# Summing eight expert rows: six on TensorE and two on VectorE, in place of four and four

## The chip, the cores and the metric

The kernel runs on one core of a Trainium2 chip. The time is the device time of one execution in microseconds (us), here the median of three. A core has several engines that run their own instruction streams and wait for each other through semaphores: TensorE (PE in the profile; its weight loads are PEld) multiplies matrices into PSUM, VectorE (DVE) and ScalarE (ACT) work element by element, GpSimd (POOL) does the gathers and scatters, and SyncE (SP) issues most of the transfers, which 16 DMA engines carry out.

## The reference

Two decoder layers over 272 tokens (16 learned meta tokens and 256 of the sequence) of width 1024. Layer 0 mixes tokens with an RWKV-7 recurrence, layer 1 with sliding-window attention. Behind each stands a mixture of experts: 64 routed ones of which every token uses 8, and a shared one. What the change touches is the end of that mixture and the norm behind it, cut to its core:

```
y = expert(x2d[tok], w_gate[e], w_up[e], w_down[e]) * gate      # 8 rows of 1024 for every token
routed = segment_sum(y, slot_tok, num_segments=T)               # their sum for every token
f = swiglu(x2d, sh_gate, sh_up, sh_down) + routed
h = layer_norm(DEEPNORM_ALPHA * h + f, ln_ffn_g[i], ln_ffn_b[i])
```

All of it is float32.

## The kernel before

The tokens stand in three tiles: tile 0 and tile 1 of 128 tokens, and a few, 16, in tile 2. Each layer runs its token mixer, then routing, then the 64 experts one after the other (their weights, 3 MB each, streamed from HBM by SyncE's queue), then the combine, which the change touches. There is no scheduler: each engine's instructions are written out in order, one block for each engine, and `Steps` objects (`end_pe`, `end_dve`, `end_act` for the combine) count what an engine has finished, so that another can wait for a named step.

The combine of a layer begins when the last scaled expert row has been scattered to a table in HBM, `routed`, with eight rows of 1024 for every token, side by side. SyncE then loads the few tokens' rows (line 1268), and for tile 0 and tile 1 the eight rows of each token in four loads of two rows each (line 1272, semaphores `routed_loaded{tile}_{pair}`): pair 0 holds rows 0 and 1, pair 3 rows 6 and 7. The eight loads are issued together, tile 0's four first. They go into the buffers `rt[t]`, which lie in the big SBUF buffer `arena`. The running sum of a tile is `h[:, t, :]`, which already holds the scaled input and the shared expert's part.

TensorE first sums the few tokens' rows (line 1851), then, for tile 0 and tile 1, adds up rows by products with the unit matrix `ident`, in two halves of 512 columns that gather in two PSUM banks for each tile (line 1857). Which rows those are is given by `ON_PE`, here rows 0, 1, 3 and 5; each row waits for its pair. The product of the last row raises the step `sum{t}` for each half.

VectorE adds the few tokens' sum and norms that tile, then takes tile 0 and tile 1 in turn: the rows of `ON_DVE_FIRST` (2 and 4) are added to `h` one after the other (line 2705, 128x1024), then the two halves from PSUM (line 2714, 128x512 each), then the rows of `ON_DVE_LAST` (6 and 7, both in pair 3), then the norm of the tile (`norm_tile`: two statistics passes on line 2683, mean and variance on 2686, two passes over the tile on 2688 and 2693; ScalarE gives the square root on line 2213). In layer 1 SyncE stores each normed tile to the output (lines 1277 to 1281), and the program ends. In layer 0 everything of layer 1's attention waits for the last norm: TensorE's transposes of `h` (line 1874, each followed by VectorE's copy on line 2732), its projections (line 1883, then line 1899 in groups, whose results ScalarE reads on lines 2250 and 2251), and the DMAs that ScalarE issues for the attention's bias (lines 2225 and 2236). SyncE's loads of the attention's weights (line 1234) do not wait for the norm, its loads of layer 1's first expert weights (line 834) do.

Of the kernel before, what the change touches and what calls it, by code (L numbers as in the profile page):

```python
# [123 lines left out]
def hybrid_trunk(nc, I, out):  # L124
    with ExitStack() as ctx:
# [3 lines left out]
        def sem(name):  # L129
            return ctx.enter_context(nc.semaphore(name))  # L130
# [18 lines left out]
        def view(at, *shape, rows=P, dt=None):  # L149
            n = int(np.prod(shape))  # L150
            assert at + n <= ARENA, (at, n)
            v = arena[0:rows, at:at + n]
            if dt is not None:
                v = v.bitcast(dt)
            if len(shape) == 2:
                v = v.rearrange("p (a b) -> p a b", a=shape[0])
            if len(shape) == 3:
                v = v.rearrange("p (a b c) -> p a b c", a=shape[0], b=shape[1])
            return v
# [93 lines left out]
        def ln_steps(t, halves=True):  # L253
# [29 lines left out]
                  for l in range(2)]  # L283
# [4 lines left out]
                            ("top8", 3), ("taken", 3), ("sel", 1), ("g0", 1), ("gsum", 1), ("g1", 1), ("g2", 1),  # L288
                            ("kr", 1), ("dest", 3), ("posm", 1), ("max", 1), ("maxi", 1), ("sm0", 1), ("sm1", 1),
                            ("sd", 6)]) for l in range(2)]  # L290
        ON_PE, ON_DVE_FIRST, ON_DVE_LAST = (0, 1, 3, 5), (2, 4), (6, 7)
        NORM = ("st0", "st1", "mv", "sub", "rec", "out")

        def norm_steps(t):
            return [(f"{n}_{t}", 1) for n in NORM]

        end_act = [Steps(sem(f"combine_act{l}"), [("std2", 1), ("std0", 1), ("std1", 1)]) for l in range(2)]
        end_pe = [Steps(sem(f"combine_pe{l}"), [("few", 2), ("sum0", 2), ("sum1", 2)]) for l in range(2)]
        end_dve = [Steps(sem(f"combine_dve{l}"), [("few", 2)] + norm_steps(2) + [("sum0", 6)] + norm_steps(0)
                         + [("sum1", 6)] + norm_steps(1)) for l in range(2)]  # L300


        NK = [128, 256, 272]
# [367 lines left out]
        few = view(16896, D)  # L671
# [1635 lines left out]
        def _(dve):  # L2307
# [280 lines left out]
            def moe(l):  # L2588
# [89 lines left out]
                def norm_tile(t):  # L2678

                    n = TILES[t][1]  # L2680
                    acc = h[0:n, t, :]
                    for half in range(2):
                        V.bn_stats(stat[0:n, t, 6 * half:6 * half + 6], acc[:, 512 * half:512 * half + 512])\
                            .then_inc(*es.step(f"st{half}_{t}"))
                    dve.wait_ge(*es.at(f"st1_{t}"))
                    V.bn_aggr(mv[0:n, t, :], stat[0:n, t, :]).then_inc(*es.step(f"mv_{t}"))
                    dve.wait_ge(*es.at(f"mv_{t}"))
                    V.scalar_tensor_tensor(out=acc, in0=acc, scalar=mv[0:n, t, 0:1], in1=lnrow[0:n, 0, :],
                                           op0=ALU.subtract, op1=ALU.mult).then_inc(*es.step(f"sub_{t}"))
                    dve.wait_ge(*end_act[l].at(f"std{t}"))  # L2690
                    V.reciprocal(rstd[0:n, t:t + 1], std[0:n, t:t + 1]).then_inc(*es.step(f"rec_{t}"))
                    dve.wait_ge(*es.at(f"rec_{t}"))
                    V.scalar_tensor_tensor(out=h[0:n, t, :], in0=acc, scalar=rstd[0:n, t:t + 1], in1=lnrow[0:n, 1, :],
                                           op0=ALU.mult, op1=ALU.add).then_inc(*es.step(f"out_{t}"))

                norm_tile(NT - 1)
                for t in range(NT - 1):
                    acc = h[:, t, :]
                    u = 0

                    def add(k):
                        dve.wait_ge(routed_loaded[t][k // 2], 16 * (l + 1))
                        if u:
                            dve.wait_ge(*es.at(f"sum{t}", u - 1))
                        V.tensor_tensor(acc, acc, rt[t][:, k, :], ALU.add).then_inc(*es.step(f"sum{t}", u))  # L2705

                    for k in ON_DVE_FIRST:
                        add(k)
                        u += 1
                    dve.wait_ge(*es.at(f"sum{t}", u - 1))  # L2710
                    for half in range(2):
                        dve.wait_ge(*end_pe[l].at(f"sum{t}", half))
                        cs = slice(512 * half, 512 * half + 512)
                        V.tensor_tensor(acc[:, cs], acc[:, cs], ps[:, 2 * t + half, :], ALU.add)\
                            .then_inc(*es.step(f"sum{t}", u))
                        u += 1
                    for k in ON_DVE_LAST:
                        add(k)
                        u += 1
                    dve.wait_ge(*es.at(f"sum{t}"))  # L2720
                    norm_tile(t)
                dve.wait_ge(*es.end())

            moe(0)


# [80 lines left out]

            dve.wait_ge(*av.end())
            moe(1)


# [24 lines left out]
```

## Time and profile before

| | |
|---|---|
| median of 3 runs | 1638.23 us (1637.66 to 1640.96) |
| the profiled execution | 1638.7 us, of which the span from first to last instruction is 1637.0 us |
| TensorE busy | 1454.8 us (89%) |
| VectorE busy | 614.0 us (38%) |
| ScalarE busy | 318.5 us (19%) |
| mean granted TensorE clock | 0.968 of full speed |
| HBM traffic | 329 GB/s over the span |

A busy share is a mean over stages with different limits, so a stage is read by its own timeline: which instruction there starts last, and what released it. In a row of the timeline the first figure is the start from the beginning of the span and the second how long the merged instructions took together; x16 means sixteen of them; the brackets give the idle time of the engine ahead of it and what ended it. TensorE's clock has two levels; 1.00 is 2.4 GHz and 0.50 is 1.2 GHz.

### The profile page before, as it was taken

To read this page: it belongs to the slowest core of one execution; us is meant where nothing else is said; L and a number is where in the kernel's file an instruction comes from. 1 tells how busy PE (TensorE), PEld (TensorE's weight loads), DVE (VectorE), ACT (ScalarE), POOL (GpSimd) and SP (SyncE) were. 2 spreads that over 40 slices of the span, in tenths; PEclk is the share of its full clock that TensorE was granted. 3 is DMA by queue.
4 is the path that set the end of the run, shared out by engine and by line. 5 is a ranking of instruction groups with operands and counts; after the bars stand their busy time and mean duration, and the time that the engine had idled before them with its cause. 6 is when DMAs were issued, how large, how long until landed. Compare 5 with 4: busy or idle time off the path is not lost.

```text
span 1637.0 us, 33339 instructions
## 1 busy us (share of the span) xinstructions
PE 1454.8 (89%) x12808; PEld 943.1 (58%) x12808; DVE 614.0 (38%) x1580; ACT 318.5 (19%) x743; POOL 328.2 (20%) x404
## 2 busy tenths in 40 slices
PE   6989988899999988888886698999999888888884
PEld 4776877656566655555553267565666555555541
DVE  5362352673333333223321704543333333333326
ACT  1621333110111111111111015111111111111110
POOL 6012000011232222222222120112322222222210
PEclk9999988899999999999999899999999999999997
DMA  7330002685999999999997995439999999999986
GB/s 201 125 116 1 4 4 80 221 324 198 414 412 412 415 416 415 415 415 415 415 415 292 370 294 206 146 126 415 413 414 414 416 414 415 415 415 416 414 346 251
DMA packets 139878, 508.42 MB, mean 311 GB/s; under 512 B 29273, under 2 KB 58273, under 8 KB 104188
## 3 DMA queue, kind: packets, MB, share of 16 engines
q1 hardware_dynamic: 103312, 456.49, 70.0%
q0 software_dynamic: 22288, 41.89, 7.1%
q10 hardware_dynamic: 14172, 8.54, 1.9%
q8 instruction: 77, 1.26, 0.3%
q14 instruction: 29, 0.24, 0.0%
HBM read 501.38 MB, written 36.90 MB: 329 GB/s over the span
## 4 chain that ended last, share of the span: by engine, by line
PE 46%; SPq 33%; DMA 8%; DVE 6%; issue 3%; ACTq 3%; ACT 1%; POOL 0%; POOLq 0%; DVEq 0%
SPq L834 33%; PE ps L782 10%; DMA arena<-in_moe_w_up 6%; PE ps L1466 6%; PE ps L800 5%; PE ps L1596 3%; ACTq L2225 3%; PE ps L763 2%; PE ps L1014 2%; PE ps L2001 2%; PE ps L770 2%; PE ps L1024 1%; DMA arena<-routed 1%; DVE h L2705 1%; PE ps L789 1%
## 5 line engine op out<-in xcount | busy, mean ns | idle before, releaser
L782 PE MATMUL ps<-arena 128*64 128x256 f32 x2752 | 316.2, 382 | 61.2 <-DMA arena<-in_moe_w_up 49.5
L782 PEld LDWEIGHTS ps<-arena 128*64 128x64 f32 x2752 | 214.2, 137 | 193.6 <-issue 126.5
L775 DVE COPY arena<-ps 128x512 f32<-128x512 f32 x128 | 88.5, 692 | 471.7 <-PE ps L770 471.7
L819 POOL DMA_INDIRECT arena<-hrows,arena x128 | 130.4, 1019 | 568.1 <-DVE arena L815 555.1
L782 PE MATMUL ps<-ring,arena 128*64 128x256 f32 x1344 | 153.5, 381 | 26.1 <-DMA ring<-in_moe_w_up 24.5
L824 POOL DMA_INDIRECT routed<-arena x128 | 117.3, 917 | 246.0 <-DVE arena L948 226.9
L800 PE MATMUL ps<-arena 128*64 128x512 f32 x688 | 166.6, 605 | 0.0
L948 DVE TENSOR_SCALAR arena<-ps,arena 64x512 f32<-64x512 f32 x128 | 95.1, 743 | 167.7 <-PE ps L800 167.7
L782 PEld LDWEIGHTS ps<-ring,arena 128*64 128x64 f32 x1344 | 99.8, 137 | 93.8 <-issue 36.4
L902 ACT COPY arena<-ps 128x256 f32<-128x256 f32 x128 | 47.7, 373 | 488.2 <-PE ps L782 488.2
L912 ACT ACTIVATE arena<-ps,arena 64x512 f32<-64x512 f32 x128 | 87.6, 684 | 208.2 <-PE ps L800 208.2
L763 PEld LDWEIGHTS ps<-arena 128*128 128x128 f32 (+1 forms) x768 | 105.6, 190 | 6.1 <-issue 2.3
L763 PE MATMUL ps<-arena 128*128 (+3 forms) x768 | 105.8, 242 | 2.1 <-DVE arena L815 2.1
L770 PE MATMUL ps<-ident,arena 128*128 128x128 f32 x512 | 83.8, 286 | 0.0
L770 PEld LDWEIGHTS ps<-ident,arena 128*128 128x128 f32 x512 | 53.8, 141 | 48.7 <-issue 48.5
L800 PE MATMUL ps<-ring,arena 128*64 128x512 f32 x336 | 81.3, 604 | 0.0
L800 PEld LDWEIGHTS ps<-arena 128*64 128x64 f32 x688 | 41.8, 136 | 63.5 <-issue 63.5
L1466 PE MATMUL ps<-arena,ring 128*128 128x272 f32 x256 | 64.2, 416 | 8.3 <-DVE arena L2379 4.4
L807 DVE SCALAR_TENSOR_TENSOR arena<-arena 128x384 f32<-128x384 f32 x128 | 69.2, 542 | 0.1
L906 ACT ACTIVATE arena<-ps 128x128 f32<-128x128 f32 x128 | 35.5, 278 | 152.4 <-PE ps L789 152.4
L1466 PEld LDWEIGHTS ps<-arena,ring 128*128 128x128 f32 x256 | 51.9, 203 | 20.4 <-DVE arena L2379 4.5
L789 PE MATMUL ps<-ident,arena 128*128 128x128 f32 x256 | 55.8, 299 | 1.0 <-issue 1.0
(360 smaller groups left out, 1532.8 us busy)
## 6 DMA issues: line engine op xcount, KB each, us to landing
arena<-in_moe_w_down SPq DMA_DIRECT2D x86, 1024.0 KB, 24.2
arena<-in_moe_w_gate SPq DMA_DIRECT2D x86, 1024.0 KB, 24.7
arena<-in_moe_w_up SPq DMA_DIRECT2D x86, 1024.0 KB, 24.8
ring<-in_moe_w_gate SPq DMA_DIRECT2D x42, 1024.0 KB, 24.6
ring<-in_moe_w_up SPq DMA_DIRECT2D x42, 1024.0 KB, 24.5
ring<-in_moe_w_down SPq DMA_DIRECT2D x42, 1024.0 KB, 24.3
arena<-routed SPq DMA_DIRECT2D x16, 1024.0 KB, 14.7
ring<-in_attn_w_qkv SPq DMA_DIRECT2D x6, 1024.0 KB, 16.4
```

Of the source, the lines that this page charges most:

```text
L763: mm = nc.tensor.matmul(dst[:, 0:3], hot[0:n, t, :], vals[0:n, t, :], start=(t == 0), stop=(t == NT - 1))
L770: mm = nc.tensor.transpose(dst[:, P * j:P * j + P], rows[:, P * j:P * j + P], ident[:, :])
L775: return nc.vector.tensor_copy(xgT.rearrange("p (r j) m -> p j r m", r=2), ps[:, bU, :].rearrange("p (j r m) -> p j r m", j=4, r=2))
L782: mm = nc.tensor.matmul(dst[SLOTS * j:SLOTS * j + SLOTS, 0:FF], xgT[:, k, :], slots[pair[j]][:, FF * k:FF * k + FF], start=(k == 0), stop= ...
L789: mm = nc.tensor.transpose(dst[:, P * j:P * j + P], guc[:, P * j:P * j + P], ident[:, :])
L800: mm = nc.tensor.matmul(dst[SLOTS * half:SLOTS * half + SLOTS, :], hid[:, j, :], slots[s][:, D * j + 512 * half:D * j + 512 * half + 512], ...
L819: return nc.gpsimd.indirect_dma_start(out=dst, out_offset=None, in_=hrows_d[l], in_offset=bass.IndirectOffsetOnAxis(ap=index, axis=0), bou ...
L824: return nc.gpsimd.indirect_dma_start(out=routed[l], out_offset=bass.IndirectOffsetOnAxis(ap=index, axis=0), in_=src, in_offset=None, boun ...
L834: sp.dma_start(slot_view(s, j), expert_weights(l, num(e))[j]).then_inc(slot_loaded[s], 16)
L912: nc.scalar.activation(ysc[q[1] % 2][:, 512:1024], ps[SLOTS:P, bY[q[1] % 2], :], ACT.Copy, scale=gate_s[q[1] % INDICES][SLOTS:P]).then_inc ...
L948: nc.vector.tensor_scalar(ysc[q[1] % 2][:, 0:512], ps[0:SLOTS, bY[q[1] % 2], :], gate_s[q[1] % INDICES][0:SLOTS], None, ALU.mult).then_inc ...
L1466: m = mm_(b[:, 0:T], slot3(s)[:, k, P * (c % 2):P * (c % 2) + P], xm[MIXBUF[mix]][:, k, :], start=(k == 0), stop=(k == KC - 1))
```

## The change

`ON_PE` becomes rows 2 to 7 and VectorE adds rows 0 and 1, both of pair 0, ahead of the halves from PSUM; nothing is added behind them, so the norm follows the halves directly. The eight loads and their order stay as they are. The number of steps that VectorE counts for a tile goes from six to four. Both layers' combines change alike. Below line 2713 the lines of the changed kernel are numbered three lower than before.

```
-        ON_PE, ON_DVE_FIRST, ON_DVE_LAST = (0, 1, 3, 5), (2, 4), (6, 7)
+        ON_PE, ON_DVE = (2, 3, 4, 5, 6, 7), (0, 1)
...
-        end_dve = [Steps(sem(f"combine_dve{l}"), [("few", 2)] + norm_steps(2) + [("sum0", 6)] + norm_steps(0)
-                         + [("sum1", 6)] + norm_steps(1)) for l in range(2)]
+        end_dve = [Steps(sem(f"combine_dve{l}"), [("few", 2)] + norm_steps(2) + [("sum0", 4)] + norm_steps(0)
+                         + [("sum1", 4)] + norm_steps(1)) for l in range(2)]
...
-                    for k in ON_DVE_FIRST:
+                    for k in ON_DVE:
                         add(k)
                         u += 1
                     dve.wait_ge(*es.at(f"sum{t}", u - 1))
...
                         V.tensor_tensor(acc[:, cs], acc[:, cs], ps[:, 2 * t + half, :], ALU.add)\
                             .then_inc(*es.step(f"sum{t}", u))
-                        u += 1
-                    for k in ON_DVE_LAST:
-                        add(k)
                         u += 1
                     dve.wait_ge(*es.at(f"sum{t}"))
                     norm_tile(t)
```

TensorE's instructions in layer 0's combine before, from the few tokens' sum to the first row of tile 1; `routed_loaded0_1` is tile 0's pair 1, and the lines of dots stand for the second halves and for second rows of the same pair:

```order
L1851 MATMUL ps<-arena,small 16x512
L1857 MATMUL ps<-arena,ident 128x512 [waits routed_loaded0_0]
L1857 MATMUL ps<-arena,ident 128x512
...
L1857 MATMUL ps<-arena,ident 128x512 [waits routed_loaded0_1]
...
L1857 MATMUL ps<-arena,ident 128x512 [waits routed_loaded0_2]
...
L1857 MATMUL ps<-arena,ident 128x512 [waits routed_loaded1_0]
```

The same place now:

```order
L1851 MATMUL ps<-arena,small 16x512
L1857 MATMUL ps<-arena,ident 128x512 [waits routed_loaded0_1]
L1857 MATMUL ps<-arena,ident 128x512
...
L1857 MATMUL ps<-arena,ident 128x512 [waits routed_loaded0_2]
...
L1857 MATMUL ps<-arena,ident 128x512 [waits routed_loaded0_3]
...
L1857 MATMUL ps<-arena,ident 128x512 [waits routed_loaded1_1]
```

TensorE's first product now waits for pair 1 in place of pair 0, a tile has twelve products in place of eight, and the last four wait for pair 3, which no product waited for before.

VectorE's instructions in layer 0's combine, from the end of the few tokens' norm to tile 0's statistics (what goes has a minus, what comes a plus; `combine_pe0` is TensorE's count of finished sums):

```order
 L2693 SCALAR_TENSOR_TENSOR h<-h,small,lnrow 16x1024 [waits combine_dve0]
-L2705 TENSOR_TENSOR h<-h,arena 128x1024 [waits routed_loaded0_1]
-L2705 TENSOR_TENSOR h<-h,arena 128x1024 [waits combine_dve0,routed_loaded0_2]
+L2705 TENSOR_TENSOR h<-h,arena 128x1024 [waits routed_loaded0_0]
+L2705 TENSOR_TENSOR h<-h,arena 128x1024 [waits combine_dve0,routed_loaded0_0]
 L2714 TENSOR_TENSOR h<-h,ps 128x512 [waits combine_pe0,combine_dve0]
 L2714 TENSOR_TENSOR h<-h,ps 128x512 [waits combine_pe0]
-L2705 TENSOR_TENSOR h<-h,arena 128x1024 [waits combine_dve0,routed_loaded0_3] x2
 L2683 BN_STATS small<-h 128x6 [waits combine_dve0]
```

The two adds ahead of the halves now wait for pair 0 alone, the two behind them are gone, and the statistics stand directly behind the halves.

## Rows read from the trace of the kernel before

**Rows 1.** The page: what the DMA engines moved, in 40 slices of the span.

```profile
GB/s 201 125 116 1 4 4 80 221 324 198 414 412 412 415 416 415 415 415 415 415 415 292 370 294 206 146 126 415 413 414 414 416 414 415 415 415 416 414 346 251
```

**Rows 2.** Timeline of layer 1's combine: start, us, engine, line, [idle before].

```profile
1603.86 3.57 PE L1851 MATMUL ps<-arena,small 128*16 128x512 f32 x4 [8.61 <-DMA arena<-routed]
...
1608.38 0.34 PEld L1857 LDWEIGHTS ps<-arena,ident 128*128 128x128 f32 x1 [0.52 <-issue]
1609.23 0.29 PEld L1857 LDWEIGHTS ps<-arena,ident 128*128 128x128 f32 x1 [0.52 <-issue]
...
1609.77 0.19 PEld L1857 LDWEIGHTS ps<-arena,ident 128*128 128x128 f32 x1 [0.24 <-issue]
1610.20 0.19 PEld L1857 LDWEIGHTS ps<-arena,ident 128*128 128x128 f32 x1 [0.24 <-issue]
...
1616.80 7.13 PE L1857 MATMUL ps<-arena,ident 128*128 128x512 f32 x16 [1.29 <-DMA arena<-routed]
...
1621.77 0.47 PEld L1857 LDWEIGHTS ps<-arena,ident 128*128 128x128 f32 x2 [0.39 <-DMA arena<-routed]
...
1623.09 2.55 DVE L2705 TENSOR_TENSOR h<-h,arena 128x1024 f32<-128x1024 f32 x2
...
1625.67 1.28 DVE L2714 TENSOR_TENSOR h<-h,ps 128x512 f32<-128x512 f32 x2
1627.06 2.56 DVE L2705 TENSOR_TENSOR h<-h,arena 128x1024 f32<-128x1024 f32 x2
1629.65 1.28 DVE L2683 BATCH_NORM_STATS2 small<-h 128x6 f32<-128x512 f32 x2
...
1632.61 1.28 DVE L2693 SCALAR_TENSOR_TENSOR h<-h,small,lnrow 128x1024 f32<-128x1024 f32 x1
```

**Rows 3.** Timeline of layer 0's combine.

```profile
897.78 3.57 PE L1851 MATMUL ps<-arena,small 128*16 128x512 f32 x4 [8.78 <-DMA arena<-routed]
...
906.05 1.98 PE L1857 MATMUL ps<-arena,ident 128*128 128x512 f32 x4 [0.28 <-DMA arena<-routed]
...
909.50 1.23 DVE L2705 TENSOR_TENSOR h<-h,arena 128x1024 f32<-128x1024 f32 x1 [2.07 <-DMA arena<-routed]
...
914.64 7.13 PE L1857 MATMUL ps<-arena,ident 128*128 128x512 f32 x16 [3.14 <-DMA arena<-routed]
...
925.64 1.29 DVE L2683 BATCH_NORM_STATS2 small<-h 128x6 f32<-128x512 f32 x2
...
929.94 6.79 PE L1874 MATMUL ps<-ident,h 128*128 128x128 f32 x24 [8.16 <-DVE h L2693]
```

**Rows 4.** Windows: us, busy (x) of PE, PEld, DVE, ACT, POOL, granted clock, DMA.

```profile
902.00:904.00 2.00, 2.00 (x5) 0.82 (x4) 1.90 (x5) 0.29 (x1) 0.00 (x0) 0.78 1.19 346
...
1609.00:1610.00 1.00, 1.00 (x3) 0.48 (x2) 0.93 (x3) 0.28 (x1) 0.00 (x0) 0.78 1.01 426
...
926.00:929.00 3.00, 0.00 (x0) 0.00 (x0) 2.90 (x6) 0.29 (x1) 0.00 (x0) 0.63 1.10 349
...
937.00:940.00 3.00, 2.53 (x3) 1.18 (x4) 0.22 (x2) 0.00 (x0) 2.92 (x2) 0.50 1.09 349
940.00:943.00 3.00, 3.00 (x8) 1.40 (x7) 0.00 (x0) 0.00 (x0) 3.00 (x2) 0.93 1.15 325
```

**Rows 5.** Timeline of the attention layer's start: ScalarE's queue and TensorE.

```profile
939.23 33.95 ACTq L2225 DMA_DIRECT2D arena<-biasd  x5
...
937.47 15.44 PE L1883 MATMUL ps<-ring,arena 128*128 128x512 f32 x32 [0.74 <-DVE arena L2732]
...
965.55 7.60 PE L1899 MATMUL ps<-arena,ring 128*128 128x272 f32 x32
974.08 2.30 PE L1899 MATMUL ps<-arena,ring 128*128 128x272 f32 x9 [0.93 <-ACT arena L2251]
```

**Rows 6.** ScalarE's DMA queue (q10), packets, MB, share: 935 to 959, 959 to 980.

```profile
q10 hardware_dynamic: 1761, 0.51, 9.9%
...
q10 hardware_dynamic: 9865, 2.91, 63.3%
```

## The prediction

> **What bounds the kernel now.** I read the page's busy shares first, then the timeline of the two places that the change touches: the combine behind layer 1's experts, which ends the program, and the one behind layer 0's, ahead of the attention layer. Over the whole span TensorE is the busiest engine, but that share says nothing here: in the last 25 us VectorE sets the pace. In layer 1 the eight loads of expert rows (1 MB each, two of a token's eight rows in each, called pairs 0 to 3 of a tile) are issued together, and TensorE, which waits for them by name, sees tile 1's pair 0 at 1616.80 and pair 2 at 1621.77 [rows 2]: one pair every 2.49 us. So tile 0's pair 1 is there at 1616.80 - 3 x 2.49 = 1609.3, and tile 1's last pair at 1624.3. From 1612.3 on VectorE's rows stand end to end; for tile 1 they are 2.55 us for two adds, 1.28 for the two halves from PSUM, 2.56 for two more adds, then the norm, with no idle time in any bracket [rows 2]. TensorE's products for tile 1 are over at 1616.80 + 7.13 = 1623.9, 1.7 us before VectorE's halves at 1625.67 ask for them. The last two adds start at 1627.06, 2.8 us after the last pair landed. So layer 1's end is VectorE's queue alone, with loads and TensorE ahead of it.
>
> In layer 0 the loads share the DMA engines with others and land later against VectorE: TensorE is released at 906.05 (tile 0's pair 1) and 914.64 (tile 1's pair 0), VectorE at 909.50 (tile 0's pair 2) [rows 3], so, at 2.49 us a pair, tile 0's pair 3 comes at about 912.1 and tile 1's pairs 1 and 3 at about 917.1 and 922.1. VectorE waits once, 2.07 us for pair 2, and is the last from 912 us on.
>
> **What it removes.** Per tile two adds on VectorE, 2.55 us. Two tiles in two layers: 10.2 us of VectorE. If VectorE stayed the bound, all of tile 1's 2.55 us and part of tile 0's would be gained at each combine's end.
>
> **What it adds.** Per tile two more rows summed on TensorE. One unit-matrix product of 128x512 is two matrix instructions in the trace (a tile's 4 rows x 2 halves stand as x16), so a tile goes from 16 to 24. Their pace at the full clock is 0.43 us each (weight loads at 1609.77 and 1610.20; x16 in 7.13 us) and 0.85 at the lower level (1608.38 and 1609.23) [rows 2]. So a pair costs TensorE 8 x 0.43 = 3.44 us while a new one lands every 2.49 us: where TensorE takes three pairs of each tile, it falls behind the loads. It also loses its start: row 0 and row 1 go to VectorE, so the first product waits for pair 1 instead of pair 0. And the order turns round: VectorE's own two adds come first, and its halves from PSUM wait for all twelve products of the tile, behind the last pair. Behind that wait stand the tile's norm, the next tile's adds, and the store or the attention layer.
>
> **Layer 1 at the full clock.** TensorE runs 48 instructions from 1609.3 without a gap (tile 1's pair 1, at 1619.3, is there when it gets to it at 1609.3 + 24 x 0.43 = 1619.6). The last ends at 1609.3 + 47 x 0.43 + 0.7 = 1630.2 (0.7 is what x16 in 7.13 leaves over 15 steps). VectorE's second half takes 0.65 and the norm starts at 1630.9, where it now starts at 1629.65 [rows 2]: 1.25 us later. VectorE itself would be ready: tile 0's halves end at about 1620.6, its norm takes 4.24 (1629.65 to 1632.61 + 1.28), two adds 2.55, so it stands ready at 1627.4. The store behind the norm shifts with it.
>
> **Layer 0 at the full clock.** From 906.05, 24 instructions bring TensorE to 916.4; it waits for tile 1's pair 1 until 917.1, and 24 more end at 917.1 + 23 x 0.43 + 0.7 = 927.7. With VectorE's second half the norm starts at 928.4, against 925.64 now [rows 3]: 2.75 us later.
>
> **The clock.** Before each combine the granted clock has fallen to 0.50, and it comes back late: in layer 0 the four products over the few tokens and the first four of tile 0 run at the lower level from 897.78, and the mean of 0.78 over 902 to 904 puts the rise at 902.9, 5.1 us later; in layer 1 the work begins at 1603.86 and the 0.78 over 1609 to 1610 puts it at 1609.4, 5.6 us later [rows 2, 3, 4]. In the attention layer it is full 2.9 us after the projections began at 937.47 (0.50 to 940, 0.93 in the next 3 us) [rows 4, 5]. These are the nearest rows for how long work on TensorE runs at 1.2 GHz after a pause: 2.9 to 5.6 us, of which half is lost, 1.4 to 2.8 us. Before, those slow steps were hidden, since TensorE was ahead; now they lie on the path. In layer 0 TensorE pauses from 901.4 to 906.05 and must start again: I take about the middle, 2.0 us, less the 0.7 us of waiting for tile 1's pair 1 that it fills: 1.3. In layer 1 the pause is only from 1607.4 to 1609.3; the loss lies between 0 (the clock rises at 1609.4 as now) and 2.8; I take 1.4, about the middle. The Trainium skill ("TensorE: Matmul & The Clock Gate", part 1) says that the low clock is the resting state and that sustained activity releases it; by that the pauses which the change opens count against it, and the trace agrees in its three late rises.
>
> **What of layer 0 reaches the end.** The attention layer starts on TensorE when layer 0's last norm is written (929.94, released by VectorE) [rows 3], and everything after it follows. The expert weights cannot make it up ahead of their stage: the DMA engines are half idle around 980 to 1100 us and only then move 415 GB/s to the end [rows 1], so that stage shifts whole. One thing takes up a little. ScalarE's queue issues the bias loads until 939.23 + 33.95 = 973.18 and only then reads its first projection; TensorE finishes its own part at 973.15 and then idles 0.93 us for ScalarE [rows 5]. Most of that issue time is not set by its start: from 935 to 959 the bias queue (q10) has 10% of the DMA time, beside weights, and only from 959 to 980 it gets 63% [rows 6]. The weight queue's work does not move with the combine until it is drained, so I expect ScalarE to end near 973.5 even when started 4 us later, and the 0.93 us goes. If ScalarE shifts as well, that is 0.
>
> **The sum.** Layer 0: 2.75 + 1.3 - 0.93 = 3.1. Layer 1: 1.25 + 1.4 = 2.65. Together 5.75 us slower. The profiled execution took 1638.7 us (span 1637.0), so 1644.45 by it; the median of the runs is 0.5 lower, which gives 1644.0. With no clock loss in either combine it is 2.75 - 0.93 + 1.25 = 3.05, with the highest and nothing taken up (2.75 + 2.8 - 0.7) + (1.25 + 2.8) = 8.9.
>
> **Rivals.**
> 1. *Layer 0's delay is swallowed in the attention layer.* TensorE's pause ahead of 929.94 is 8.16 us now [rows 3] and would be about 5.2 (only VectorE's half and the norm between). If the clock stays up over it, the transposes (6.79 us now [rows 3], at the lower clock, at most halved) and the first projections give back up to 3.4 + 1.4 = 4.8 us, until ScalarE's 973.2 is the bound: layer 0 then adds nothing and the total is 2.65, 1640.9. Against it: TensorE's last product of layer 0 ends at 914.64 + 7.13 = 921.8 [rows 3], and the mean of 0.63 over 926 to 929 puts the clock's fall at 926.8, 5.0 us later [rows 4], so 5.2 us just reaches a fall; for it, the 3.14 us pause ahead of 914.64 brought none. 8%.
> 2. *Faster: the products keep up with the loads.* The place is TensorE's pace in line 1857. Setting 1609.3 + 47 x + 0.7 + 0.7 equal to 1629.65, the change gains in layer 1 as soon as a step costs less than 0.40 us. At half the step, 0.215, TensorE is done 0.4 + 8 x 0.215 = 2.1 us after the last pair lands (1626.4), layer 1 gains 2.5, layer 0 about 0.6 (922.1 + 2.1 + 0.8 = 925.0), and the time is 1635.1. Against it stand twice fifteen steps of 0.43 at the full clock in this very line, x16 in 7.13 us in either layer [rows 2, 3]. The Trainium skill's figure for back-to-back products of 512 columns ("TensorE: Matmul & The Clock Gate", "Back-to-back issue gap") is 216 ns, half of what these rows show for float32; the measured step decides. 4%.
> 3. *VectorE's adds are the wait.* If VectorE reached tile 1's halves later than TensorE, the loss would be smaller; it has 2.8 us in hand at 1627.4 and about 3 in layer 0 (tile 0's halves end at 917.2, its norm and two adds 6.8 us later at 924.0), so I give it nothing of its own.
>
> **How the numbers follow.** My forecast, TensorE as the bound of both combines, has 88%; its own range, from no clock loss to the highest, is 1641.3 to 1647.1. What a measurement of this kernel can tell from no change is 0.2%, 3.3 us, so slower by more than that begins at 1641.5; 3% of the forecast's chance falls under it. Slower 0.85; same 0.11 (the 3%, and rival 1); faster 0.04. The range is taken a little wider for the attention layer's own clock, which may rise up to 1.5 us later or earlier than now: 1640.6 to 1647.5.
>
> **What would show it.** Right: in the profile after, each tile's products stand as x24; VectorE idles ahead of each tile's halves, 4 to 9 us for tile 0 and 2 to 5 for tile 1 (line 2714 released by TensorE's line 1857), and the halves start within 0.1 us of the products' end; in layer 1 the norm of tile 1 starts 1.2 to 4 us later than 1629.65, in layer 0 it starts 2.7 to 4.8 us later than 925.64; TensorE's 0.93 us before the third group of line 1899 is gone. Wrong: if VectorE has no idle time in front of line 2714, the products are not the bound and rival 2 holds; if the attention layer's third group of line 1899 still starts near 974, rival 1 holds; if the loads land at other times than these rows, the whole working falls, since TensorE's start is read from them.

## The result and the profile after

The changed kernel takes 1649.55 us (median of 12 runs, 1641.89 to 1657.21), the kernel before beside it 1641.69 (12 runs, 1637.31 to 1650.9). The ratio is 1.0047 [1.0028, 1.0066]: 7.7 us slower, between 4.6 and 10.8. The direction is as forecast, and the forecast step (5.75 us, a ratio of 1.0035) lies within the interval; the time of 1649.55 lies outside the range of 1640.6 to 1647.5. One run of the twelve lies inside it, and the profiled run (1647.58 us, span 1645.9) just outside.

Runs of one kernel differ by more than the change, so the traces are compared by stretches inside them. Each combine starts with SP's issue of the load of the few tokens' rows (L1268). In the trace before:

```profile
894.31 0.35 SPq L1268 DMA_DIRECT2D arena<-routed  x1
...
1600.47 0.35 SPq L1268 DMA_DIRECT2D arena<-routed  x1
```

From there to tile 1's statistics a combine took 925.64 - 894.31 = 31.33 us in layer 0 and 1629.65 - 1600.47 = 29.18 in layer 1 [rows 2, 3]. After, layer 0's timeline (start, us, engine, line, [idle before]):

```profile
896.86 0.35 SPq L1268 DMA_DIRECT2D arena<-routed  x1
900.26 3.57 PE L1851 MATMUL ps<-arena,small 128*16 128x512 f32 x4 [8.76 <-DMA arena<-routed]
...
908.57 22.65 PE L1857 MATMUL ps<-arena,ident 128*128 128x512 f32 x48 [4.73 <-DMA arena<-routed]
...
920.17 1.48 DVE L2714 TENSOR_TENSOR h<-h,ps 128x512 f32<-128x512 f32 x2 [8.93 <-PE ps L1857]
...
930.47 1.48 DVE L2714 TENSOR_TENSOR h<-h,ps 128x512 f32<-128x512 f32 x2 [2.08 <-PE ps L1857]
931.98 1.28 DVE L2683 BATCH_NORM_STATS2 small<-h 128x6 f32<-128x512 f32 x2
936.28 6.79 PE L1874 MATMUL ps<-ident,h 128*128 128x128 f32 x24 [5.06 <-DVE h L2693]
...
943.81 16.92 PE L1883 MATMUL ps<-ring,arena 128*128 128x512 f32 x32 [0.74 <-DVE arena L2729]
...
972.74 0.47 ACT L2250 ACTIVATE arena<-ps,arena 128x256 f32<-128x256 f32 x1 [38.90 <-PE ps L1910]
...
973.37 17.00 PE L1899 MATMUL ps<-arena,ring 128*128 128x272 f32 x73
```

and layer 1's:

```profile
1606.33 0.35 SPq L1268 DMA_DIRECT2D arena<-routed  x1
...
1615.14 22.64 PE L1857 MATMUL ps<-arena,ident 128*128 128x512 f32 x48 [1.40 <-DMA arena<-routed]
...
1626.74 1.48 DVE L2714 TENSOR_TENSOR h<-h,ps 128x512 f32<-128x512 f32 x2 [5.58 <-PE ps L1857]
...
1637.04 1.48 DVE L2714 TENSOR_TENSOR h<-h,ps 128x512 f32<-128x512 f32 x2 [2.08 <-PE ps L1857]
1638.55 1.29 DVE L2683 BATCH_NORM_STATS2 small<-h 128x6 f32<-128x512 f32 x2
```

Where x16, with waits for loads between, stood before [rows 2, 3], now 48 instructions run without a gap: both tiles' products form one block, begun when pair 1 has landed (11.71 us after the load's issue in layer 0, 8.81 in layer 1; before, TensorE was released by pair 1 at 906.05 - 894.31 = 11.74, so pair 1 lands where it did; the later pairs land while TensorE is still behind, so no wait shows them). VectorE waits for TensorE ahead of every pair of halves, where it had no idle time before. The stretches are 35.12 and 32.22 us: 3.79 and 3.04 longer.

The granted clock under these blocks (windows: us, busy (x) of PE, PEld, DVE, ACT, POOL, granted clock, DMA share, GB/s; 0.50 is 1.2 GHz, 1.00 is 2.4 GHz):

```profile
908.00:912.00 4.00, 3.43 (x4) 1.51 (x5) 3.14 (x3) 0.00 (x0) 0.00 (x0) 0.50 1.03 431
912.00:914.00 2.00, 2.00 (x6) 0.90 (x5) 0.00 (x0) 0.00 (x0) 0.00 (x0) 0.95 0.97 410
...
943.00:949.00 6.00, 5.26 (x7) 2.19 (x7) 0.46 (x2) 0.00 (x0) 5.75 (x3) 0.50 1.05 397
...
1610.00:1618.00 8.00, 6.43 (x8) 1.75 (x9) 4.76 (x8) 0.29 (x1) 0.00 (x0) 0.50 1.01 422
```

At the full clock 48 steps take 20.8 us (seen in some runs below), so each block loses 1.8 us to the lower level. The third low stretch is the attention layer's projections, 16.92 us where they took 15.44 [rows 5].

From layer 0's load to the end of the span (called the tail from here on) the trace before has 1637.0 - 894.31 = 742.7 us, the one after 1645.9 - 896.86 = 749.0: +6.3. The other 2.55 us by which the load itself comes later after (896.86 against 894.31) lie ahead of all that the change touches, and are there already at the first product with expert weights, 382.5 before and 384.9 after.

### The profile page after: what moved, and what is told of

It is laid out like the page before. It is cut to its first block, busy times and chain, and to the rows that moved or that the text cites. A ratio compares the mean times of both kernels' runs of the same rounds, so it can differ in the third digit from the quotient of the medians.

```text
span 1645.9 us, 33387 instructions
## 1 busy us (share of the span) xinstructions
PE 1472.6 (89%) x12840; PEld 951.9 (58%) x12840; DVE 604.7 (37%) x1572; ACT 318.5 (19%) x743; POOL 327.2 (20%) x404
## 4 chain that ended last, share of the span: by engine, by line
PE 51%; SPq 33%; DMA 8%; DVE 4%; issue 3%; ACT 1%; ACTq 0%; POOL 0%; POOLq 0%; DVEq 0%
SPq L834 33%; PE ps L782 10%; DMA arena<-in_moe_w_up 6%; PE ps L1466 6%; PE ps L800 5%; PE ps L1857 3%; PE ps L1596 3%; PE ps L763 2%; PE ps L1014 2%; PE ps L1899 2%; PE ps L2001 2%; PE ps L770 2%; PE ps L1024 1%; DMA arena<-routed 1%; PE ps L789 1%
```

## The experiments

Theory A: TensorE, at 3.44 us a pair against 2.49 us between landings, started late by rows 0 and 1 on VectorE, and slowed by the clock, sets the end of both combines, and the attention layer passes layer 0's delay on. Rival B: the count of products alone is what costs. Rival C: the lower clock is what costs. In the measures below the two numbers of a kernel are its stretches in layer 0 and layer 1 (from L1268's issue to tile 1's statistics); the kernel before has 31.33 and 29.18, the changed one 35.12 and 32.22. Kernels listed together ran beside the same runs of the kernel before: e1 to e4 beside 35 of them (median 1644.31 us), e5 to e8 beside 27 (1642.19), e9 to e11 beside 29 (1645.56).

**Six rows on TensorE, but the early ones (e1).** The count of products stays, the start and VectorE's place change.

```
-        ON_PE, ON_DVE = (2, 3, 4, 5, 6, 7), (0, 1)
+        ON_PE, ON_DVE = (0, 1, 2, 3, 4, 5), (6, 7)
```

> Six rows stay on TensorE, but they are rows 0 to 5 (pairs 0 to 2), and VectorE adds rows 6 and 7 ahead of the halves. Compared is the stretch from the issue of the few tokens' load to the first statistics pass over tile 1: 31.3 us in layer 0 and 29.2 in layer 1 before the change, 35.1 and 32.2 after it. Theory (the products start a pair late and run behind the loads): with pair 0 as the start TensorE begins 4.7 and 1.9 us earlier, its slow steps fall into the wait for pair 1, and the stretches come back to 31 to 32 us and 29.5 to 30; the time is within 0.1% of before. Rival (twelve products a tile are too many wherever they stand): the stretches stay at 35 and 32 and the time at +0.4%.

Ratio 0.9986 [0.9968, 1.0003], 1642.81 us; stretches 31.68 and 29.69. Layer 1's timeline:

```profile
1612.08 0.35 SPq L1268 DMA_DIRECT2D arena<-routed  x1
1618.92 22.09 PE L1857 MATMUL ps<-arena,ident 128*128 128x512 f32 x48
...
1640.26 1.48 DVE L2714 TENSOR_TENSOR h<-h,ps 128x512 f32<-128x512 f32 x2 [2.00 <-PE ps L1857]
```

The same 48 instructions begin 6.84 us after the load's issue in place of 8.81 and cost nothing that the timing shows. So B falls: it is not the 16 more instructions of a combine (48 in place of 32), but which pairs they wait for. TensorE is still the last in layer 1 (2.00 us of idle time ahead of the halves), only 2 us earlier.

**Four rows on TensorE, but the late ones (e6).** The counter-test: no product more than before, all of them from pairs 2 and 3.

```
-        ON_PE, ON_DVE = (2, 3, 4, 5, 6, 7), (0, 1)
+        ON_PE, ON_DVE = (4, 5, 6, 7), (0, 1, 2, 3)
...
-... ("sum0", 4) ... ("sum1", 4) ...
+... ("sum0", 6) ... ("sum1", 6) ...
```

> Four rows on TensorE as before, but in the order of the change: TensorE takes rows 4 to 7 (pairs 2 and 3), VectorE adds rows 0 to 3 ahead of the halves. Theory (what costs is the late start and the wait for halves behind the last pair; with four rows VectorE, with two adds more in its queue behind that wait, is the last): layer 0's stretch 34 to 36 us, layer 1's 29.6 to 31.3. Rival (the loss is the 24 instructions a tile): 31.3 and 29.2 as before the change.

Ratio 1.0044 [1.0019, 1.0069], as slow as the change; stretches 36.55 and 32.71, above what both theories expected. Layer 0's timeline and its clock:

```profile
926.50 9.81 PE L1857 MATMUL ps<-arena,ident 128*128 128x512 f32 x16 [8.20 <-DMA arena<-routed]
```

```profile
918.00:921.00 3.00, 0.30 (x1) 0.00 (x0) 2.56 (x5) 0.29 (x1) 0.00 (x0) 0.96 1.04 338
921.00:932.00 11.00, 5.50 (x7) 2.41 (x8) 7.02 (x7) 0.00 (x0) 0.00 (x0) 0.53 1.00 416
```

The order alone costs as much as the whole change. The miss of size is the clock: behind the few tokens' products it was back (0.96 over 3 us in which TensorE worked for 0.30), and it had fallen again (0.53) when the products began after 8.20 us of waiting, so x16 took 9.81 us in place of 7.13. In layer 1 the 32 products took 17.08 us, where twice x16 at the full clock are 14.3.

**The change in layer 1 alone (e3).** `ON_PE` and the rest become tuples per layer, layer 0 as before.

```
+        ON_PE, ON_DVE_FIRST, ON_DVE_LAST = ((0, 1, 3, 5), (2, 3, 4, 5, 6, 7)), ((2, 4), (0, 1)), ((6, 7), ())
...
-                    for k in ON_PE:
+                    for k in ON_PE[l]:
```

> The change in layer 1's combine alone; layer 0's is that of before. Theory (each combine pays by itself): layer 0's stretch 31.3 us, layer 1's 31.8 to 32.8, the attention layer as before with TensorE idle 0.9 us for ScalarE, the time 1.001 to 1.0025 of before. Rival (the loss is made in layer 0 and its consequences, layer 1 follows it only): the time is that of before.

Ratio 1.0013 [0.9988, 1.0038]: the timing can't tell it from no change. Stretches 32.53 and 30.28, the second below the 31.8 to 32.8 that were expected, and the first above its 31.3. In this profiled run layer 1's products ran at the full clock from their first step:

```profile
1614.20 20.87 PE L1857 MATMUL ps<-arena,ident 128*128 128x512 f32 x48 [1.39 <-DMA arena<-routed]
```

The loss against the trace before is 30.28 - 29.18 = 1.10 us, where the working had 1.25 at the full clock. Layer 0, whose code is that of before, took 1.2 us longer than in the trace before: its clock fell as tile 1's products began, and x16 took 8.83 us in place of 7.13. At the third group of line 1899's products only 0.28 us of this are left (80.05 us after L1268's issue against 79.77), and TensorE no longer waits for ScalarE there.

**Spare products against the clock.** `keep_busy` is a helper of the kernel that multiplies a unit matrix by the router's weights into a bank that nobody reads. The changed kernel gets some ahead of the few tokens' sum and some between it and the first row; only spare work is added. Twice: e2 with 9 and then 6 (layer 0) or 3 (layer 1), e5 with 5 or 6 and then 4 or 2.

```
+                keep_busy(SPARE_BANK[0], 9)
... (the few tokens' products)
+                keep_busy(SPARE_BANK[0], (6, 3)[l])
```

> The changed kernel with products whose result nobody reads (into a spare PSUM bank) in TensorE's pauses of both combines: nine ahead of the few tokens' sum, then six in layer 0 and three in layer 1 ahead of tile 0's first product. Theory (part of the loss is steps at the lower clock): all 48 products of a combine run at 0.43 us, the stretches are 31.3 + 2.75 = 34.1 us in layer 0 and 29.2 + 1.25 = 30.4 in layer 1, against 35.1 and 32.2. Rival (the clock plays no part, the loss is the order of the work): 35 and 32 as in the changed kernel.

> The spare products of the second experiment again, but fewer (five and four in layer 0, six and two in layer 1), since there they ran past the landing of pair 1 and held up the first real product. Theory (about 1.8 us a combine are steps at the lower clock): the 48 products of each combine take 20.8 us in place of 22.65, start within 0.3 us of pair 1's landing, and the stretches from the few tokens' load to tile 1's statistics are 33.3 to 34.1 us in layer 0 and 30.4 to 30.8 in layer 1, against 35.1 and 32.2; from layer 0's load of the few tokens to the end of the span 746 us, against 749.0 after the change and 742.7 before. Rival (spare products only move the wait): 35 and 32, and 749.

e2: ratio 1.0038 [1.0018, 1.0058], stretches 35.33 and 31.98. e5: 1.0031 [1.0005, 1.0058], stretches 36.05 and 31.06; the tails are 749.2 and 748.6, no shorter than the change's 749.0 by more than tails vary, where 746 was expected of e5. e2's timelines of both layers:

```profile
897.79 0.35 SPq L1268 DMA_DIRECT2D arena<-routed  x1
...
906.34 5.42 PE L1005 MATMUL ps<-router,ident 128*128 128x512 f32 x12
911.60 20.76 PE L1859 MATMUL ps<-arena,ident 128*128 128x512 f32 x48
...
1607.71 0.35 SPq L1268 DMA_DIRECT2D arena<-routed  x1
...
1618.07 20.87 PE L1859 MATMUL ps<-arena,ident 128*128 128x512 f32 x48 [0.85 <-DMA arena<-routed]
```

The block of 48 takes 20.76 and 20.87 us: against 22.65 and 22.64, so 1.8 to 1.9 us of the change's cost in each combine are the clock's. But the expected gain did not come: in layer 0 the spare products ran past pair 1's landing, and in layer 1 pair 1 landed 10.36 us after the load's issue, not 8.81. In e5 the shorter filling kept to time, but in layer 0 the few tokens' rows came 5.33 us after the issue (3.40 in the changed kernel) and the clock fell all the same:

```profile
908.65 0.35 SPq L1268 DMA_DIRECT2D arena<-routed  x1
913.98 1.89 PE L1852 MATMUL ps<-arena,small 128*16 128x512 f32 x4 [3.29 <-DMA arena<-routed]
...
921.38 22.56 PE L1859 MATMUL ps<-arena,ident 128*128 128x512 f32 x48 [1.87 <-DMA arena<-routed]
```

Where both worked, in e5's layer 1, the stretch is 31.06, 1.16 shorter than the change's. C explains a part (1.8 us a combine) and not the rest. Why loads landed 1 to 2 us later in two of these four combines, and in none of the other kernels, is open.

**Five rows on TensorE, three on VectorE.** TensorE takes both rows of pair 0 and one of pairs 1 to 3, so it starts early and has half as much to do for each late pair.

```
-        ON_PE, ON_DVE = (2, 3, 4, 5, 6, 7), (0, 1)
+        ON_PE, ON_DVE = (0, 1, 3, 5, 6), (2, 4, 7)
...
-... ("sum0", 4) ... ("sum1", 4) ...
+... ("sum0", 5) ... ("sum1", 5) ...
```

> TensorE sums five rows (0, 1, 3, 5, 6), VectorE adds three (2, 4, 7) ahead of the halves. Theory (VectorE was the bound of layer 1's combine by the length of its own queue, and TensorE had time in hand): layer 1's stretch falls by one add for each tile, 2.5 us, to 26.7; layer 0's is 30.5 to 31.3, and of that nothing reaches the end since ScalarE's bias loads end at 973 as before; the time 0.998 to 0.9995 of before. Rival (any product more puts TensorE behind the loads): layer 1's stretch is 30 us or more and the time is not below before.

> Five rows on TensorE and three on VectorE once more. Theory: from layer 0's load of the few tokens to the end of the span 739.5 to 741 us against 742.7, a ratio of 0.997 to 0.9995. Rival (its first trace had a lucky clock in the attention layer): 742 or more and a ratio of 1.

e4: ratio 0.9988 [0.9966, 1.0009], stretches 30.75 and 27.05. Again as e10: 0.9969 [0.9939, 0.9998], stretches 30.61 and 27.10. Tile 1's last row on each engine in e4's layer 1:

```profile
1635.33 1.23 DVE L2705 TENSOR_TENSOR h<-h,arena 128x1024 f32<-128x1024 f32 x1 [0.56 <-DMA arena<-routed]
1635.35 1.98 PE L1857 MATMUL ps<-arena,ident 128*128 128x512 f32 x4 [0.54 <-DMA arena<-routed]
```

Both engines now wait for the last pair (0.56 and 0.54 us, by DMA) and share it, and the halves follow with no idle time (1636.59): in this trace the loads are the bound. In e10's, tile 1's three adds run without a wait:

```profile
1630.57 3.88 DVE L2705 TENSOR_TENSOR h<-h,arena 128x1024 f32<-128x1024 f32 x3
```

There VectorE's own queue is the last, at the same length. Layer 1's combine is 2.1 us shorter than in the first trace of before in both (1.7 than in the second, e12 below, with 28.80). The tails are 739.7 and 738.0 against 742.7, e10's below the 739.5 to 741 that were expected. By the times it is ahead of the kernel before in both measurements, by 0.1% and 0.3%; only the second interval, and that of e8, which has the same split, lie below 1, so the gain is small and its size uncertain.

**Spare products ahead of the attention layer.** Five of them behind layer 0's last product, on the changed kernel (e7, e11) and on the five and three (e8).

```
+            keep_busy(SPARE_BANK[0], 5)
```

> The changed kernel with five spare products behind layer 0's last unit-matrix product, in TensorE's pause of 5.1 us ahead of the attention layer's transposes; the combine is untouched. Theory (TensorE bounds the attention layer's start after the change, half of it at the lower clock, and ScalarE's bias loads are over 8 us before TensorE comes to need them): the transposes and first projections run at the full clock and the third group of projections starts 3 to 6 us earlier, so from layer 0's load of the few tokens to the end of the span it is 743 to 746 us against 749.0. Rival (ScalarE's queue or VectorE's copies bound it): 748.5 to 749.

> Five rows on TensorE and three on VectorE as in the fourth experiment, with the five spare products ahead of the attention layer's transposes. Theory (with the shorter combine ScalarE's bias loads end within 1 us of TensorE's second group of projections, so TensorE cannot gain): from layer 0's load of the few tokens to the end of the span 738.7 to 739.7 us, against 739.7 without them. Rival (the clock is worth as much here as in the seventh experiment): 734 to 737.

> The changed kernel with five spare products ahead of the attention layer's transposes, once more, since its trace gave 743.1 us from layer 0's load of the few tokens to the end and its six timed runs a ratio of 1.0073. Theory (the trace is right and those runs were slow ahead of the combine): 743 to 746 us again and a ratio below that of the changed kernel on this chip, 1.000 to 1.003. Rival (the spare products cost more in most runs than the trace shows): the ratio is again at or above that of the changed kernel.

In e7's trace the clock stays up, and the transposes and projections take 5.08 and 13.97 us in place of 6.79 and 16.92:

```profile
936.92 5.08 PE L1875 MATMUL ps<-ident,h 128*128 128x128 f32 x24 [0.77 <-DVE h L2694]
...
942.74 13.97 PE L1884 MATMUL ps<-ring,arena 128*128 128x512 f32 x32 [0.73 <-DVE arena L2730]
```

```profile
930.00:950.00 20.00, 18.50 (x56) 9.63 (x55) 9.50 (x21) 0.29 (x1) 8.78 (x6) 1.00 1.08 368
```

The third group of line 1899's products starts 79.57 us after L1268's issue, where it starts at 83.95 after the change and 974.08 - 894.31 = 79.77 before: layer 0's whole delay is taken up, and the tail is 743.1 us. So the mechanism of rival 1 exists; the change alone doesn't set it off. But the times went against this trace: ratio 1.0073 [1.0039, 1.0107] over 6 runs. The repetition gave 1.0014 [0.9987, 1.0042] over 12 and, in its trace, a clock that fell during the projections (16.17 us) and a tail of 746.6, just above the 743 to 746 expected. Whether these spare products gain any time is open.

e8: ratio 0.9970 [0.9945, 0.9996], 1640.15 us, stretches 30.75 and 26.50, tail 739.9 where e4 had 739.7. The expected reason for no gain was ScalarE's bias loads, and TensorE does wait for ScalarE in its trace:

```profile
947.24 34.49 ACTq L2226 DMA_DIRECT2D arena<-biasd  x5
...
982.63 3.68 PE L1900 MATMUL ps<-arena,ring 128*128 128x272 f32 x15 [0.90 <-ACT arena L2252]
```

The clock fell in this run too (0.69 over 934 to 950), so what a full clock there would be worth is not tested by it.

**The change and the kernel before again.** No edit. So far one trace of each stood for its kernel.

> The changed kernel once more, for a second trace of it and for more runs beside the kernel before on the same chip. From layer 0's load of the few tokens to the end of the span the first traces gave 742.7 us before and 749.0 after. Theory (the combines and the attention layer's start make the whole loss, and the spread between runs comes from ahead of layer 0's combine): 746.5 to 750 here, wherever the span as a whole ends, and a ratio near 1.004. Rival (the change also slows something ahead of the combine, or the first trace was a poor draw): the ratio is above 1.006 or below 1.002, and the stretch is not above 746.

> The kernel before once more, for a second trace of it. Theory (the spread between runs is made ahead of layer 0's combine, and the first trace of before was a fast draw there): from layer 0's load of the few tokens to the end of the span 741.5 to 744 us as in the first trace (742.7), while the first expert product starts later than the first trace's 382.5 us, at 385 to 400. Rival (the first trace was a fast draw behind that point too, so that the loss by the change is smaller than it looks): 745 us or more.

e9: 1.0032 [1.0001, 1.0064], 1651.0 us, stretches 35.76 and 32.17, tail 749.4, as expected. The clock over layer 0's combine:

```profile
911.00:915.00 4.00, 0.95 (x2) 0.00 (x0) 3.07 (x6) 0.29 (x1) 0.00 (x0) 0.92 0.93 304
915.00:922.00 7.00, 5.27 (x7) 2.22 (x8) 4.22 (x5) 0.00 (x0) 0.00 (x0) 0.51 1.02 421
```

As in e6 it was up only over the pause that the late start opens (0.92 with 0.95 us of work in 4 us) and down again when the products began.

e12: 1638.3 us, in one run, beside one of 1653.36 of the same kernel: 15 us between two runs of one program. Its tail, 742.4 us, agrees with the first trace's 742.7, as expected. Its first product with expert weights does not come later, as expected, but at 382.9 us. What is new in it is layer 0's combine:

```profile
894.22 0.35 SPq L1268 DMA_DIRECT2D arena<-routed  x1
...
914.54 10.14 PE L1857 MATMUL ps<-arena,ident 128*128 128x512 f32 x16 [3.15 <-DMA arena<-routed]
...
928.10 1.29 DVE L2683 BATCH_NORM_STATS2 small<-h 128x6 f32<-128x512 f32 x2
```

The clock fell in the 3.15 us ahead of tile 1's products, x16 took 10.14 us, and the stretch is 33.88 us, 2.55 more than in the first trace. So the kernel before isn't free of the clock's cost either. The tail doesn't show it, because other parts of it vary: from the third group of line 1899 to the next layer's first product with expert weights it is 113.4 us here and 114.7 in the first trace, and lies between 113.3 and 115.1 in all fourteen traces with no order by kernel. Tails are thus good to about 1 us, stretches of a combine to the clock's part in them.

## Why the prediction was right in its mechanism and wrong in its time

**Bound and pace: right.** TensorE bounds both combines; VectorE idles 8.93 and 2.08, 5.58 and 2.08 us ahead of the halves, within the 4 to 9 and 2 to 5 that were named. The step is 0.43 us (20.87 / 48 = 0.435), the start is pair 1's landing, and that landing stands where it stood. Rival 2 (products that keep up) falls with the step, rival 3 with the idle times.

**The cost in the combines: right in sum.** In layer 0 the forecast was 2.75 + 1.3 = 4.05 and the two first traces show 3.79; in layer 1 it was 1.25 + 1.4 = 2.65 and they show 3.04. Over all traces that have the same code in a combine: layer 0 with the change 35.12, 35.76, 35.12, 35.66 (mean 35.42), without it 31.33, 33.88, 32.53 (32.58): +2.8; layer 1 with it 32.22, 32.17, 30.48, 32.27, 30.28 (31.48), without it 29.18, 28.80 (28.99): +2.5. Layer 0's mean lies 1.2 below the forecast because the code of before pays for the clock there too in two of its three traces (33.88 and 32.53); the forecast was read from the one in which it does not, and against that one the mean is 4.1 longer. Layer 1's clock term, forecast at 1.4 as about the middle of 0 to 2.8, is no middle value in the runs: the stretch is 30.3 to 30.5 when the clock is up in time, and 32.2 when it is not. The full-clock part of 1.25 is borne out by the two traces with the clock up, 1.10 in e3 and 1.30 in e7; layer 0's, 2.75, was never measured by itself. The order as the cause, more than the count, stands on e1 and e6.

**The 0.93 us: right.** TensorE's wait ahead of the third group of line 1899 is gone (973.37, x73 with no bracket), and ScalarE reads its first projection at 972.74, 0.56 us earlier than the 973.30 that it had before, though it started 6.3 us later: its bias loads' end did not move with the combine. e3 shows the same slack with nothing changed in layer 0: a combine longer by 1.2 us arrives as 0.28.

**Rival 1: wrong here, and for the reason given against it.** The clock fell in the pause ahead of 936.28 (0.50 over 943 to 949), and the third group starts 83.95 - 79.77 = 4.2 us later. Between the second traces it is less, 83.27 - 82.04 = 1.2 us, since e12's combine paid for the clock itself. Had the clock stayed up, it would have been right, as e7's trace shows. One argument in its favour, that a pause of 3.14 us brought no fall, doesn't hold beyond that trace: in e12 3.15 us did.

**Mis-sized: the attention layer's own clock.** It was left out of the sum and put into the range as up to 1.5 us either way. In the first trace of the change it came at the upper end: the projections lost 16.92 - 15.44 = 1.48 us. With 3.79, -0.93 and 3.04 that makes 7.4; the tail shows 6.3, since the stretches between took about 1 us less, which is within what tails vary by. In the second trace of the change (e9) the projections took 15.60 us, in that of the kernel before (e12) 16.25, so these four traces show no loss here that goes with the change.

**The step that failed: "the median of the runs is 0.5 lower, which gives 1644.0".** The sum was laid on the profiled run and three runs of 1637.66 to 1640.96, as if they were the kernel's time. They were low: twelve runs, these three among them, have a median of 1641.69, the nine others one of 1643.95, and the 91 that ran beside the experiments one of 1643.6, from 1635.5 to 1656.3, with a standard deviation of 5.0. On 1641.69 the same 5.75 us make 1647.4, and the range, moved up by the same 3.5 us, holds 1649.55. Why the three were low the record does not show. The range failed by the same step: it held the unknown costs of the change and nothing of the spread between runs; at 6.9 us it is narrower than half of the 15.3 us over which the twelve runs after lie. Of the 5.6 us by which 1649.55 misses 1644.0, 3.5 are the base (1641.69 against the 1638.23 that was used) and 2.1 the size (the medians differ by 7.9, against 5.75; the interval of 4.6 to 10.8 holds both).

What the spread is made of can be read in part. The time goes with the mean granted clock: over the twelve runs after, 1641.89 us is the run with 0.969 and 1657.21 the one with 0.960 (correlation -0.89); over the 91 of the kernel before it is -0.91. In the fourteen traces the first product with expert weights comes between 382.5 and 400.0 us, and layer 0's combine always 511 to 512.5 us behind it. Line 782's first and last starts and the windows up to it, in e6, the latest:

```profile
L782 PE MATMUL ps<-ring,arena x1344: 379/379/431, 400.0 to 1587.2; 128*64 128x256 f32 x192
```

```profile
5.00:380.00 375.00, 338.07 (x5134) 261.20 (x5135) 171.91 (x380) 103.03 (x225) 49.56 (x92) 0.90 0.34 115
```

and in e12, among the earliest:

```profile
L782 PE MATMUL ps<-ring,arena x1344: 379/379/430, 382.9 to 1566.3; 128*64 128x256 f32 x192
```

```profile
5.00:380.00 375.00, 337.54 (x5195) 265.10 (x5196) 178.79 (x413) 102.79 (x226) 52.52 (x95) 0.94 0.35 116
```

So up to 17 us arise ahead of the first product with expert weights, where nothing was changed (it is layer 0's token mixer for the most part), with the granted clock lower over it (0.90 against 0.94). An estimate from these rows, 0.04 of 375 us, gives 15 us of TensorE's full speed that was not granted, which is near the 17; why the clock is lower in one run than in another the traces do not show. That a long run of the unchanged kernel loses them there as well is likely and was not seen: both its profiled runs were short ones. For the same reason it stays open whether the two traces of before, the earliest of the fourteen, are so by chance; its other runs left no trace.

## What to carry to other kernels

Before work is moved to the engine that has idle time, two things are to be read: whether that engine can still begin with the data that lands first, and whether it does a piece in less time than lies between two landings. Here a pair took 3.44 us against 2.49 between landings. With the first pair taken away from TensorE its idle time turned into the bound; with the first pair left to it, six rows neither gained nor lost clearly (e1). A split in which both engines share the last pair shortened layer 1's combine (27.1 us in place of 29.2). A late start also opens a pause, and the clock that falls in it is paid on the path. And before a range is drawn around a sum of a few microseconds, the spread between runs of the same program belongs in it; a few runs that agree don't show it, and within one trace the length of a stage between two fixed events is the better measure.

## What the runs showed of the hardware

Behind the few tokens' products the granted clock was up over a stretch in which TensorE had little to do, and had fallen again when the next block began: 0.92 and then 0.51 in e9, 0.96 and then 0.53 in e6. After pauses of 3.14 and 3.15 us ahead of the same products in the same code it stayed up once (7.13 us for x16) and fell twice (10.14 in e12, 8.83 in e3). Two traces of one program can therefore differ by 2.5 us in one combine with nothing changed.
